# RWKV gate product as four tiles inside the recurrence, with both factors from partition 0, and one bonus sum per chunk

## The reference

```python
p  = rms(x) @ W_in
y_mla  = MLA(p[:, :, :MLA_IN])
y_rwkv = RWKV7(p[:, :, MLA_IN:])
x += concat(rms(y_mla)*beta_a, rms(y_rwkv)*beta_r) @ W_out
```

```python
g = jax.nn.sigmoid(g_l) @ g2                 # g_l: 256 tokens x 160, g2: 160 x 512
state = state * w_t + (state @ a_t) b_t + v_t k_t     # one token after another, 8 heads of 64 x 64
y = groupnorm(state @ r_t) * gn_gain + gn_bias
bonus = jnp.sum(r * k * r_k, axis=-1, keepdims=True) * v
y = (y + bonus) * g
```

## Time and profile before

| | us |
|---|---|
| median of 3 runs | 1171.42 |
| lowest, highest run | 1171.36, 1176.49 |
| span of the traced execution | 1174.9 |
| TensorE busy | 1150.5 |
| VectorE busy | 799.6 |
| ScalarE busy | 561.2 |

### The profile page before, as it was taken

The page is one execution under the profiler, slowest core; times in us unless marked ns, Lnnn a source line. Parts: engine busy times, 40 slices in busy tenths (PEclk is TensorE's granted clock), DMA queues, the critical chain, the costliest instruction groups (busy, mean ns, idle before and its releaser), DMA issues.

```text
span 1174.9 us, 27231 instructions
## 1 busy us (share of the span) xinstructions
PE 1150.5 (98%) x10722; PEld 1062.9 (90%) x10724; DVE 799.6 (68%) x1462; ACT 561.2 (48%) x991; POOL 1.7 (0%) x10
## 2 busy tenths in 40 slices
PE   7999999999999999999999999999999999999998
PEld 6999999999978799999989999989999788999997
DVE  4666667888634976666686666677885468666665
ACT  4444444586333544444454444465843344444443
POOL 0000000000000000000000000000000000000000
PEclk8999999999998999999999999999999999999999
DMA  6666665744000366666556666666520014666663
GB/s 188 200 188 183 182 191 166 186 129 127 4 2 1 115 201 186 181 189 183 183 158 187 190 179 189 185 165 171 144 93 4 3 49 133 196 190 183 184 191 125
DMA packets 243958, 173.41 MB, mean 148 GB/s; under 512 B 14428, under 2 KB 228596, under 8 KB 243892
## 3 DMA queue, kind: packets, MB, share of 16 engines
q1 hardware_dynamic: 243892, 172.46, 50.1%
HBM read 171.39 MB, written 1.05 MB: 147 GB/s over the span
## 4 chain that ended last, share of the span: by engine, by line
PE 83%; DVE 10%; ACT 4%; issue 1%; DMA 1%; SPq 0%; ACTq 0%; DVEq 0%
PE bank L1347 23%; PE bank L1348 23%; PE bank L1349 22%; PE bank L1360 9%; DVE wlo L803 2%; DVE xlo L832 1%; PE bank L1354 1%; ACT whi L527 1%; PE bank L1486 1%; DMA raw<-in_ffn_w_gate_dram 1%; ACT work L642 0%; DVE xtok L1318 0%; PE bank L1485 0%; PE bank L1661 0%; DVE work L972 0%
## 5 line engine op out<-in xcount | busy, mean ns | idle before, releaser
L803 DVE TENSOR_TENSOR wlo<-raw,whi 128x1024 fp32r<-128x1024 f32 (+1 forms) x322 | 392.5, 1220 | 242.1 <-ACT whi L527 241.6
L1347 PE MATMUL bank<-xhi,whi 128*128 128x256 f32 x1696 | 484.3, 286 | 5.7 <-DVE xlo L832 4.9
L1348 PE MATMUL bank<-xlo,whi 128*128 128x256 f32 x1696 | 480.4, 283 | 0.0
L1349 PE MATMUL bank<-xhi,wlo 128*128 128x256 f32 x1696 | 480.3, 283 | 0.0
L527 ACT ACTIVATE whi<-raw 128x1024 fp32r<-128x1024 f32 (+1 forms) x322 | 338.7, 1052 | 291.6 <-PE bank L1349 261.4
L1347 PEld LDWEIGHTS bank<-xhi,whi 128*128 128x128 f32 x1696 | 325.5, 192 | 12.8 <-issue 7.4
L1348 PEld LDWEIGHTS bank<-xlo,whi 128*128 128x128 f32 x1696 | 325.7, 192 | 3.7 <-issue 0.5
L1349 PEld LDWEIGHTS bank<-xhi,wlo 128*128 128x128 f32 x1696 | 325.5, 192 | 0.0
L1347 PE MATMUL bank<-whi,hhi 128*128 128x512 f32 x352 | 138.7, 394 | 1.1 <-DVE hlo L918 1.0
L1348 PE MATMUL bank<-wlo,hhi 128*128 128x512 f32 x352 | 138.0, 392 | 0.0
L1349 PE MATMUL bank<-whi,hlo 128*128 128x512 f32 x352 | 137.0, 389 | 0.0
(11 more groups left out here) (222 smaller groups left out, 1038.0 us busy)
## 6 DMA issues: line engine op xcount, KB each, us to landing
raw<-in_ffn_w_gate_dram SPq DMA_DIRECT2D x88, 512.0 KB, 3.8
raw<-in_ffn_w_up_dram SPq DMA_DIRECT2D x88, 512.0 KB, 3.8
raw<-in_ffn_w_down_dram SPq DMA_DIRECT2D x88, 512.0 KB, 3.5
raw<-in_w_in_dram SPq DMA_DIRECT2D x32, 512.0 KB, 3.9
raw<-in_w_out_dram SPq DMA_DIRECT2D x16, 512.0 KB, 3.6
raw<-in_w_q_up_dram SPq DMA_DIRECT2D x4, 384.0 KB, 3.2
xtok<-in_x_dram SPq DMA_DIRECT2D x4, 256.0 KB, 5.3
raw<-in_w_in_dram SPq DMA_DIRECT2D x4, 256.0 KB, 4.1
```

The lines of the kernel that those rows point to most:

```text
L803: V_.tensor_tensor(wlo[:, b.slot, 0:width], raw[:, b.slot, 0:width], whi[:, b.slot, 0:width].bitcast(F32), ALU.subtract).then_inc(lo_ready, 1)
L1347: mm(out, hi, mhi, start=start, stop=False, **kw)
L1348: mm(out, hi, mlo, start=False, stop=False, **kw)
L1349: return mm(out, lo, mhi, start=False, stop=stop, **kw)
```

## The change

The gate product becomes four tiles, one per chunk. In chunks 0 and 1 the tile stands after `u{c}`, in chunks 2 and 3 after `x{c}`. The second factor of a tile, which was 32 rows at partition 64, becomes 96 rows from partition 0; the 64 added rows of the weights are zero, so the sum is the same. They stand in a buffer of their own, `g2b`, that GpSimd clears once at the start. ScalarE copies each tile for itself into `gT`. The bonus sums are made one after `y0` and one after `y1`, both in bank 1, so the second waits until VectorE has used the first; VectorE uses them after `x1` and after `x2`. `bonus` moves from unit 11 to unit 15. `pT1`, which writes bank 7 again, waits for the last gate copy and no longer for a bonus.

```diff
-         + ["x0", "u0", "s0"] + max_steps(0) + ["x1", "u1", "sa1", "s1"] + max_steps(1)
-         + ["ye0", "x2", "bonus0", "bonus1", "u2"] + max_steps(2) + ["sa2", "s2", "x3", "u3"] + max_steps(3)
+         + ["x0", "u0", "s0"] + max_steps(0) + ["x1", "bonus0", "u1", "sa1", "s1"] + max_steps(1)
+         + ["ye0", "x2", "bonus1", "u2"] + max_steps(2) + ["sa2", "s2", "x3", "u3"] + max_steps(3)
...
+        g2b = sb("g2b", [96, RW])
...
-        rT, kT, vT, zl, ta, lc, kk, sc, einv, kmod, gT, bonus = (unit(i) for i in range(12))
+        rT, kT, vT, zl, ta, lc, kk, sc, einv, kmod, gT = (unit(i) for i in range(11))
+        bonus = unit(15)
...
-        g2a, g2b = unit(11)[:, 0:RW], unit(11)[:, RW:2 * RW]
+        g2a = unit(11)[:, 0:RW]
...
+            pool.memset(g2b[0:64, :], 0.0).then_inc(once, 1)
...
-                def kept_gate(j):
-                    act.wait_ge(mix_pe.sem, mix_pe.at(l, f"gup_{j}"))
-                    nc.scalar.activation(gT[:, 512 * j:512 * (j + 1)], bank[7][:],
-                                         ACT.Copy).then_inc(mix_act.sem, mix_act.step(f"gT{j}"))
+                def kept_gate(i):
+                    act.wait_ge(mix_pe.sem, mix_pe.at(l, f"gup_{i}"))
+                    nc.scalar.activation(gT[:, SEQ * i:SEQ * (i + 1)], bank[7][:, SEQ * (i % 2):SEQ * (i % 2 + 1)],
+                                         ACT.Copy).then_inc(mix_act.sem, mix_act.step(f"gT{i}"))
...
                 exps(1)
+                kept_gate(2)
                 exps(2)
+                kept_gate(3)
                 kept_prob(0)
...
-                    if c == 2:
-                        bonus_half(0), bonus_half(1)
+                    if c in (1, 2):
+                        bonus_half(c - 1)
...
-                def gate_half(j):
-                    if j:
-                        pe.wait_ge(mix_act.sem, mix_act.at(l, "gT0"))
+                def gate_tile(i):
+                    if i:
+                        pe.wait_ge(mix_act.sem, mix_act.at(l, f"gT{i - 1}"))
                     else:
                         pe.wait_ge(mix_act.sem, mix_act.at(l, "Q3_1"))
                         pe.wait_ge(mix_dve.sem, mix_dve.at(l, "gs1"))
-                    for i in (2 * j, 2 * j + 1):
-                        o = bank[7][:, SEQ * (i % 2):SEQ * (i % 2 + 1)]
-                        mm(o, g2a[:, P * i:P * (i + 1)], lora[:, 1, :], start=True, stop=False)
-                        ins = mm(o, g2b[64:96, P * i:P * (i + 1)], lora[64:96, 2, :], start=False, stop=True)
-                    ins.then_inc(mix_pe.sem, mix_pe.step(f"gup_{j}"))
+                    o, n = bank[7][:, SEQ * (i % 2):SEQ * (i % 2 + 1)], slice(P * i, P * (i + 1))
+                    mm(o, g2a[:, n], lora[:, 1, :], start=True, stop=False)
+                    mm(o, g2b[:, n], lora[0:96, 2, :], start=False, stop=True).then_inc(mix_pe.sem,
+                                                                                       mix_pe.step(f"gup_{i}"))
...
                 def bonus_sum(b):
-                    if b == 0:
-                        pe.wait_ge(mix_act.sem, mix_act.at(l, "gT1"))
-                        pe.wait_ge(mix_dve.sem, mix_dve.at(l, "rk"))
-                    mm(bank[1 if b else 7][:], con("onesbd"), kmod[:, 512 * b:512 * (b + 1)], start=True,
+                    pe.wait_ge(mix_dve.sem, mix_dve.at(l, "bonus0" if b else "rk"))
+                    mm(bank[1][:], con("onesbd"), kmod[:, 512 * b:512 * (b + 1)], start=True,
                        stop=True).then_inc(mix_pe.sem, mix_pe.step(f"bsum_{b}"))
...
                     if c < 2:
                         scores(c)
+                    else:
+                        gate_tile(c)
...
-                    if c == 0:
-                        gate_half(0)
-                    if c > 1:
+                    if c < 2:
+                        gate_tile(c)
+                    else:
                         scores(c)
...
-                    if c == 0:
-                        gate_half(1)
-                    if c == 1:
-                        bonus_sum(0), bonus_sum(1)
+                    if c < 2:
+                        bonus_sum(c)
```

More of the change, by code:

```diff
@@ L237 @@
          + pair("Q0") + pair("Q1") + pair("pc4") + pair("Q2") + pair("Q3") + pair("pc5")
-         + ["gT0", "ex0", "gT1", "ex1", "ex2", "pT0", "ex3", "gsq", "pT3", "pT4", "pT5", "yhi0", "yhi1", "ysq0", "yhi2", "yhi3", "ysq"]
+         + ["gT0", "ex0", "gT1", "ex1", "gT2", "ex2", "gT3", "pT0", "ex3", "gsq", "pT3", "pT4", "pT5", "yhi0", "yhi1", "ysq0", "yhi2", "yhi3", "ysq"]
          + [f"yhi{4 + j}" for j in range(HP)] + ["rsq"])
@@ L373, in build @@
                                                                        MIX_A), Steps(sem("mix_pe"), MIX_P)
-        ONCE = 6
+        ONCE = 7
         def quarter(phase, i):
@@ L1208, in bonus_half @@
                     s = slice(512 * b, 512 * (b + 1))
-                    V_.tensor_tensor(bonus[:, s], bank[1 if b else 7][:], vT[:, s], ALU.mult).then_inc(mix_dve.sem, mix_dve.step(f"bonus{b}"))
+                    V_.tensor_tensor(bonus[:, s], bank[1][:], vT[:, s], ALU.mult).then_inc(mix_dve.sem, mix_dve.step(f"bonus{b}"))
                 def kept_y(b):
@@ L1297, in mixing @@
                 dve.wait_ge(mix_dve.sem, mix_dve.at(l, "gb"))
-                dve.wait_ge(mix_act.sem, mix_act.at(l, "gT1"))
+                dve.wait_ge(mix_act.sem, mix_act.at(l, "gT3"))
                 V_.tensor_tensor(yN, yN, gT, ALU.mult).then_inc(mix_dve.sem, mix_dve.step("gm"))
@@ L1719, in turned_prob @@
                     if i == 1:
-                        pe.wait_ge(mix_dve.sem, mix_dve.at(l, "bonus0"))
+                        pe.wait_ge(mix_act.sem, mix_act.at(l, "gT3"))
                     if i > 1:
```

## The result

The changed kernel takes 1171.18 us in the median of 22 runs; the kernel before, run beside it, 1174.92. The ratio of the two, taken over all their runs, is 0.9975 (95% interval 0.9965 to 0.9985): 2.9 us faster, within the 0.5% that the prediction called no change. The median of before had been 1171.42 in the three runs shown ahead of the prediction; in 22 and later in 27 and 29 runs it is 1174.92, 1173.83 and 1173.76. So three runs had fallen on the low side, and the predicted 1169.1 started 2.3 to 3.5 us too low.

The account below looks back on a forecast made before the run. TensorE's program order was taken as the bound: per layer 5.02 + 1.92 + 1.79 - 4.24 - 2.12 - 1.22 = 1.15 us less, 2.3 for two layers, so 1171.4 to 1169.1 us; range 1168.2 to 1174.4.

Parts of the forecast that it names:

- The bound: Recurrence of each layer: TensorE works in program order, 98% busy, so whatever leaves its order shortens the span.
- Gate tiles, 1.06 us: Gate product on TensorE: each tile's pair overlaps and takes 1.06 us, four 4.24, against 5.02 before, per layer.
- rival B: Gate product: the pair does not overlap, a tile takes 1.25 us; 0.38 us gained a layer, 1170.7 us; chance 0.20.
- The three stalls, 1.79 us: TensorE's waits for VectorE copies before s1, u2 and u3, 0.60 us each, vanish under gate tiles.
- the new wait, 1.22: Scores of chunk 1 on TensorE wait 1.22 us for ScalarE's exponentials of chunk 0, a stall not there before.
- Bonus sums apart, 2.12: The two bonus sums on TensorE, made separately, cost 1.06 us each, together 2.12, against 1.92 as a pair.
- the edits at nothing: Extra ScalarE gate copies, moved VectorE bonus uses and GpSimd's memset cost nothing, hidden by other work; tightest cover 0.4 us.
- The base: Whole kernel: the gain of 2.3 us is taken from the three-run median, 1171.4 to 1169.1 us.
- E: Recurrence: the stalls only move, through late bank copies or other waits; no change, 1171.4 us; chance 0.08.
- A: The main forecast: gate pairs overlap, 1.15 us less a layer in the recurrence, 1169.1 us; chance 0.45.
- C: Median falls on an execution with layer 0's 1.2 GHz stretch, 4.5 to 5.1 us more, about 1174; chance 0.20.
- D: Wait before scores 1 drops TensorE to 1.2 GHz in the recurrence; 1178.1 us in both layers, 1173.6 in one; chance 0.07.

Follow-up runs that it names:

- e1: The kernel before with only the gate product's second factor over 96 rows from partition 0; median 1172.32 us, ratio 0.9989 to the kernel before.
- e2: The changed kernel with each gate tile's second factor again over 32 rows from partition 64; median 1173.12 us, ratio 0.9989 to the kernel before.
- e5: The changed kernel with VectorE taking the score maxima of chunks 0 and 1 before the state copies; median 1170.05 us, ratio 0.9959 to the kernel before.
- e4: The changed kernel with chunk 1 reordered on TensorE, gate tile before the scores, bonus sum after u1; median 1174.15 us, ratio 0.9999 to the kernel before.
- e3: The changed kernel with the four gate tiles' second factors over 32 or 64 rows, from partition 0 or 64; one run, 1171.5 us.
- e8: The changed kernel itself run again beside the kernel before and three others; median 1170.97 us, ratio 0.9972 to the kernel before.

## Why the prediction was right, point by point

**The bound.** TensorE's order in the recurrence sets the time: e1, e2 and e5 moved the stretch by what their terms said, within 0.02 us. e4 fell short by 0.6: its terms counted TensorE's order alone, and a wait for ScalarE appeared at scores 2.

**Gate tiles, 1.06 us.** Right in size, and the rows matter as much as the place: rival B is e2, 26.92. The reason given for 1.06 was wrong. The prediction took it from the start at partition 0; e3 shows that 32 and 64 rows from 0 do not overlap and 96 do. Both reasons gave the same number here, since the change alters start and count at once: that the right bound was taken was partly luck. Rows of before could have told them apart: the 64-row loads behind the scores start at partition 0 and are late (under e3). For the same reason the argument of rival B, that the gate pair is the only one of unlike row counts, overlooked these steps.

**The three stalls, 1.79 us, and the new wait, 1.22.** Right: all three brackets are gone, and scores 1 wait 1.29 us by the load's bracket, which holds about 0.07 of ordinary spacing. The sum 1.15 a layer stands against 1.14 measured in both layers.

**Bonus sums apart, 2.12, and the edits at nothing.** Each sum takes its 1.06 us (the first from 331.92 to 332.98 us), and the stretch leaves no room for another cost. Bonus 1 ends at 344.21, u2's matmuls feed VectorE only from 344.86: the tight place held.

**The base.** The step that was off is the one that carried the gain over to a median: 1171.42 was the median of three runs, and the kernel lies at 1173.8 to 1174.9. The gain in the comparison, 2.9 us, is 0.6 more than forecast, within its interval (1.8 to 4.1), and 2.06 at equal clock. The time itself speaks less for the forecast than the trace does: 1171.18 lies 2.1 us above 1169.1 and nearer to rivals B (1170.7) and E (1171.4). From the base of 22 runs the same 2.3 us would have given 1172.6. It is the stretch of 26.15 us, and not the median, that singles out A.

**Rivals.** C did not come true for the median, but what it feared is real: the traces show falls in the softmax stretch in some executions, in layer 0, layer 1 or both, and the run times have these levels; the median of the changed kernel lies with the runs at the high clock. D did not happen: the clock is 1.00 through the recurrence, across the wait before scores 1. E did not: TensorE has no wait there that the forecast had not counted.

## What to carry to other kernels

Before filling a stall on the busiest engine with work from elsewhere, look at what that work had been covering: here two gate halves hid the path of the exponentials, and 1.2 of 1.8 us came back as a wait for them. A wait for ScalarE can be VectorE's order: taking the maxima as soon as their input is there removed it at no cost in the stretch. And where the clock has levels, settle an edit of 1 us by the stretch that it touches, in one trace at one clock, and compare run times at equal clock.

## What the runs showed of the hardware

- A float32 matmul of 256 columns on 96 rows, 64 of them zeros, is cheaper behind one on 128 rows than one on 32 or 64 rows: the pair takes 1.06 us against 1.25, because its first weight load runs under the pass before it (0.32 us behind the first load, against 0.63). Behind 96 rows it is the same: the next 96-row load comes after 0.33 us, a 64-row load after 0.63. From which count above 64 this holds, and whether 96 rows from another start do it, was not tried.
- The same program at the same place sometimes falls to 1.2 GHz and sometimes doesn't. Five of the ten traces have a fall in the softmax stretch, six falls in all, and each comes 1.7 to 2.4 us after the sixteen two-column matmuls begin (before 366.3 after 364.1 us, changed 941.2 after 939.2, e8 942.3 after 939.9, e4 366.2 after 364.5). A short one (half clock for about 3.4 us) costs 1.3 us, a long one (10.3 us) 4.5.
